# Six opening transfers on another queue, two norm sums two chunks later, and the mixers' last three units two steps later

## The reference

```python
for l in range(2):                                   # first block
    hn = rms_norm(h, norm_mix_g[l])
    q, k, v, xr, gate = split(hn @ w_in[l])
    o_attn = diff_attention(rope(norm(q)), rope(norm(k)), v, lam)
    o_rec = rg_lru_branch(xr, gate, ...)
    h = h + concat(o_attn, o_rec) @ w_out[l]
    hn = rms_norm(h, norm_ffn_g[l]);  h = h + (silu(g) * u) @ w_down[l]
for l in range(2):                                   # second block
    # mixer: short convolution, top-k attention ("d"), chunk-band attention ("c")
    mix = hybrid_mixer(x, positions, w_in[l], conv_w[l], rel_bias[l], w_mix_out[l])
    x = layer_norm(ALPHA * x + mix)
    cross = memory_cross_attention(x, mem, w_mq[l], w_mkv[l], w_mo[l])
    x = layer_norm(ALPHA * x + cross)                # the second norm
    x = layer_norm(ALPHA * x + squared_relu_mlp(x, w_ff1[l], w_ff2[l]))
```

## Time and profile before

| | before |
|---|---|
| time, three runs | 2864.87, 2864.66 and 2860.75 us (median 2864.66) |
| profiled execution | 2860.26 us, span 2858.5 us |
| TensorE busy | 2768.6 us, 97% of the span |
| VectorE, ScalarE, GpSimd busy | 1651.1, 1268.0 and 370.8 us |
| DMA | 85 GB/s on average |

### The profile page before, as it was taken

How to read it: one execution, slowest core, us unless ns; L and a number is a source line. 1 busy time by engine, 2 the same in 40 slices (tenths; PEclk the granted TensorE clock), 3 DMA queues, 4 the chain that set the end, 5 groups by cost and what they waited for, 6 DMA issues and landing times.

```text
span 2858.5 us, 39044 instructions
## 1 busy us (share of the span) xinstructions
PE 2768.6 (97%) x15748; PEld 2346.3 (82%) x15752; DVE 1651.1 (58%) x2479; ACT 1268.0 (44%) x2133; POOL 370.8 (13%) x291
## 2 busy tenths in 40 slices
PE   8999999999989999999999999999999999999997
PEld 7878999999877788887668888888776688888886
DVE  6786545454777745454876466333658764653335
ACT  5574322224674422233564545333445644443333
POOL 2222000001222000000223120000312231200003
PEclk9999999999999999999999999999999999999999
DMA  4112232232112233332123223323221232233332
GB/s 145 52 45 67 89 91 90 94 90 83 51 45 74 93 96 97 102 94 88 56 75 126 89 67 96 98 94 97 84 81 61 77 126 82 67 104 96 95 97 67
DMA packets 71923, 244.36 MB, mean 85 GB/s; under 512 B 9152, under 2 KB 10816, under 8 KB 71744
## 3 DMA queue, kind: packets, MB, share of 16 engines
q1 hardware_dynamic: 66528, 235.50, 25.7%
q10 hardware_dynamic: 5216, 6.36, 0.7%
HBM read 239.73 MB, written 2.10 MB: 85 GB/s over the span
## 4 chain that ended last, share of the span: by engine, by line
PE 83%; DVE 11%; ACT 3%; issue 2%; POOL 0%; DMA 0%; SPq 0%; ACTq 0%; DVEq 0%
PE psum L578 23%; PE psum L584 23%; PE psum L581 23%; PE psum L650 2%; DVE temp L2194 1%; DVE weights_hi_lo L1757 1%; PE psum L1080 1%; PE psum L673 1%; PE psum L675 1%; PE psum L1092 1%; PE psum L677 1%; DVE small L2192 1%; PE psum L907 1%; PE psum L935 1%; PE psum L960 1%
## 5 line engine op out<-in xcount | busy, mean ns | idle before, releaser
L578 PE MATMUL psum<-act_hi_lo,weights_hi_lo 128*128 128x264 f32 (+2 forms) x2544 | 776.3, 344 | 3.7 <-ACT temp L1290 2.8
L581 PE MATMUL psum<-act_hi_lo,weights_hi_lo 128*128 128x264 f32 (+2 forms) x2544 | 750.9, 334 | 1.9 <-DVE weights_hi_lo L1757 1.9
L584 PE MATMUL psum<-act_hi_lo,weights_hi_lo 128*128 128x264 f32 (+2 forms) x2544 | 752.1, 335 | 0.0
L1181 ACT ACTIVATE weights_hi_lo<-weights_float 128x1024 fp32r<-128x1024 f32 (+2 forms) x446 | 463.7, 1042 | 499.1 <-PE psum L584 430.7
L1757 DVE TENSOR_TENSOR weights_hi_lo<-weights_float,weights_hi_lo 128x1024 fp32r<-128x1024 f32 (+2 forms) x446 | 557.5, 1251 | 219.4 <-ACT weights_hi_lo L1181 218.1
L578 PE MATMUL psum<-hidden_hi_lo,weights_hi_lo 128*128 128x512 f32 (+2 forms) x1584 | 519.6, 358 | 3.7 <-DVE x_residual L2010 1.4
L584 PE MATMUL psum<-hidden_hi_lo,weights_hi_lo 128*128 128x512 f32 (+2 forms) x1584 | 511.6, 353 | 1.4 <-DVE hidden_hi_lo L2020 1.4
L581 PE MATMUL psum<-hidden_hi_lo,weights_hi_lo 128*128 128x512 f32 (+2 forms) x1584 | 511.2, 352 | 1.3 <-DVE weights_hi_lo L1757 1.3
L578 PEld LDWEIGHTS psum<-act_hi_lo,weights_hi_lo 128*128 128x128 f32 x2544 | 439.7, 189 | 68.3 <-issue 17.7
L584 PEld LDWEIGHTS psum<-act_hi_lo,weights_hi_lo 128*128 128x128 f32 x2544 | 438.4, 188 | 48.1
L581 PEld LDWEIGHTS psum<-act_hi_lo,weights_hi_lo 128*128 128x128 f32 x2544 | 438.0, 188 | 47.9 <-issue 2.6
(11 more groups left out here) (290 smaller groups left out, 3297.5 us busy)
## 6 DMA issues: line engine op xcount, KB each, us to landing
weights_float<-in_w_ff SPq DMA_DIRECT2D x128, 512.0 KB, 3.6
weights_float<-in_w_gu SPq DMA_DIRECT2D x88, 512.0 KB, 3.6
weights_float<-in_w_in SPq DMA_DIRECT2D x70, 512.0 KB, 3.6
weights_float<-in_w_down SPq DMA_DIRECT2D x32, 448.0 KB, 3.3
weights_float<-in_w_out SPq DMA_DIRECT2D x16, 512.0 KB, 3.6
weights_float<-in_w_down SPq DMA_DIRECT2D x16, 512.0 KB, 3.5
weights_float<-in_w_mv SPq DMA_DIRECT2D x16, 512.0 KB, 3.2
weights_float<-in_w_mix SPq DMA_DIRECT2D x16, 512.0 KB, 3.3
```

The costliest lines, as they stand in the source:

```text
L578: e.matmul(slot[:, place:place + c1 - c0], w_hi[:, col], x_hi[:, c0:c1], start=first, stop=False)
L581: e.matmul(slot[:, place:place + c1 - c0], w_lo[:, col], x_hi[:, c0:c1], start=False, stop=False)
L584: mm = e.matmul(slot[:, place:place + c1 - c0], w_hi[:, col], x_lo[:, c0:c1], start=False, stop=final)
L1181: e.activation(K.parts(n)[0][:, 0:cols], K.staged(n)[:, 0:cols], ACT.Copy).then_inc(*K.did("hi", n))
```

## The change

Three things. First, the six transfers (rotary tables, constants, the causal mask, lambda's vectors, the recurrent gates, the second block's parameters) go from ScalarE's queue to SP's, behind x and the first three w_v pieces and ahead of the fourth; GpSimd makes its masks behind the sums of squares; `small_before` stands behind all low parts of x, `scalar_small` at step 1 and `small_after` at step 2 of the first attention. Second, in `tiles_high_first` five chunks instead of three stand ahead of `between()`. Third, the "d" units with i = 3 stand two steps later, at 91, 94 and 96.

```diff
-          + [("d", p, i, 67 + (5 * n) // 2) for n, (i, p) in enumerate((i, p) for i in range(4) for p in range(3))])
+          + [("d", p, i, 67 + (5 * n) // 2 + (2 if i == 3 else 0)) for n, (i, p) in enumerate((i, p) for i in range(4) for p in range(3))])
...
-    high(group[:-1], order[:3])
+    high(group[:-1], order[:5])
     between()
     B.clear(2 * group[-1][1], 2 * group[-1][1] + 1)
-    high(group[-1:], order[:3])
-    high(group, order[3:])
+    high(group[-1:], order[:5])
+    high(group, order[5:])
...
     e.dma_start(m["x"][:, :, 0:META], t["meta_t"]).then_inc(*did("landed_meta", by=16))
     e.dma_start(m["par1"][:, :, :], t["params1"]).then_inc(*did("landed_params", by=16))
-    e.dma_start(m["rope"][:, 0:2, :], t["consts"][:, C_COS1:C_COLS].rearrange("p (a n) -> p a n", a=2)).then_inc(
-        *did("landed_rope", by=16))
-    e.dma_start(m["consts"][:, :], t["consts"][:, 0:C_CAUSAL]).then_inc(*did("landed_consts", by=16))
-    e.dma_start(K.once[:, 0:2 * P], t["consts"][:, C_CAUSAL:C_COS1]).then_inc(*did("landed_once", by=16))
-    e.dma_start(K.lams[:, 0:DEPTH * 4 * HEAD_DIM], t["lambdas"]).then_inc(*did("landed_lams", by=16))
-    e.dma_start(K.gates, t["w_gates"][0]).then_inc(*did("landed_gates", 0, by=16))
-    e.dma_start(m["par2"][:, :, :], t["params2"]).then_inc(*did("landed_params2", by=16))
...
     for s in range(STEPS1):
+        if l == 0 and s == 1:
+            scalar_small(e, w, K, 0)
         if s == 2:
...
     split_lo(e, w, K, 1)
     next_lo(e, w, K, "a", 0, 2)
-    small_before(e, w, K, 0)
     next_lo(e, w, K, "a", 0, 3)
     split_lo(e, w, K, 2)
     for k in range(4, DC):
         next_lo(e, w, K, "a", 0, k)
-    small_after(e, w, K, 0)
+    small_before(e, w, K, 0)
...
+        if l == 0 and s == 2:
+            small_after(e, w, K, 0)
         if s - 2 in UNIT_AT1[l]:
...
     square_sums(e, w, K, "a", 0, T1)
+    pool_masks(e, w, K)
     for l in range(DEPTH):
```

More of the change, by code:

```diff
@@ L1743, in scalar_program @@
     scalar_start(e, w, K)
-    scalar_small(e, w, K, 0)
     for l in range(DEPTH):
@@ L2491, in pool_start, with pool_masks @@
     e.memset(K.v[:, 4, :], 0.0).then_inc(*did("meta_zero"))
+def pool_masks(e, w, K):
+    m, did, done = K.m, K.did, K.done
     w.wait_ge(*done("landed_consts"))
@@ L2642, in sync_program @@
             load(c // 2)
+    e.dma_start(K.lams[:, 0:DEPTH * 4 * HEAD_DIM], t["lambdas"]).then_inc(*did("landed_lams", by=16))
+    e.dma_start(m["consts"][:, :], t["consts"][:, 0:C_CAUSAL]).then_inc(*did("landed_consts", by=16))
+    e.dma_start(K.gates, t["w_gates"][0]).then_inc(*did("landed_gates", 0, by=16))
+    e.dma_start(m["rope"][:, 0:2, :], t["consts"][:, C_COS1:C_COLS].rearrange("p (a n) -> p a n", a=2)).then_inc(
+        *did("landed_rope", by=16))
+    e.dma_start(K.once[:, 0:2 * P], t["consts"][:, C_CAUSAL:C_COS1]).then_inc(*did("landed_once", by=16))
+    e.dma_start(m["par2"][:, :, :], t["params2"]).then_inc(*did("landed_params2", by=16))
     for n in range(STAGING, len(PIECES)):
```

## The result

The changed kernel takes 2871.15 us in the median of 7 runs (2867.16 to 2872.71), the kernel before in the same comparison 2861.30 us (7 runs, 2859.14 to 2864.87). The ratio is 1.0027, with a 95% interval of 1.0017 to 1.0037: slower by 0.27%, some 8 us, or 9.9 us from median to median. The prediction was 2863.2 us, in 2856 to 2869; the time lies outside, on the slow side.

A forecast was written before the change was run, and what follows sets the result against it. TensorE, busy for 97% of the span, was taken as the bound, so time could come only from its idle stretches and clock. Start −2.2, norm −3.4, mixers +3.2, clock +3.0 gave +0.6 on 2862.6: 2863.2 us, range 2856 to 2869.

The forecast's parts named there:

- part 2: Second norm: eight more rows ahead of the sums remove TensorE's wait in both layers, −3.4 us (−2.5 to −3.5).
- The forecast of the sums: Second norm: 1.92 us of rows cover the 1.74 us idle, so the wait goes and the sums come 0.18 later.
- The correction: Behind w_ff1's first group: reads the squared mean and root many rows later, so the 0.18 us delay was given no cost.
- Part 3: Mixers: old waits go, −2.8 us a layer; a new 4.4 us wait for bank 0's emptying comes; both layers +3.2.
- Part 4: TensorE's clock: falls to half behind each new mixer wait, 1.5 us a layer, +3.0 us (0 to 5.5).
- Part 1: Start and first attention: earlier first matmul −1.2, fourth w_v piece's wait −1.1, later small operations +0.1, sum −2.2 us.
- The first matmul: Start: comes at 7.5 us instead of 8.70, a gain of 1.2 us (0.8 to 1.5).
- The tiny operations in the attention: First attention, step 2: `small_after`, 4.9 us on VectorE against 4.51 idle, costs TensorE +0.1 us, +0.4 without cover.
- The wait of L675: Fourth w_v piece: TensorE's 1.07 us wait for the low part behind `small_after` goes, −1.1 us.
- Rival 3: Mixers: half clock lasts 5.5 us instead of 3.4 at each of two places, +3.1, 2865.7 us; chance 0.2.
- the second low stretch of the earlier trace: At 2065.40 to 2070.90 us: half clock under full work for 5.50 us, taken as support for the longer half clock.
- all cases: The forecast (0.38) and four rivals: clock stays up 0.2, no new wait 0.12, longer half clock 0.2, start gains nothing 0.1.

The follow-up runs named there:

- the run of the norm alone: Only five chunks instead of three ahead of the second norm's sums, against the kernel before: 2865.79 us beside 2864.51, ratio 1.0007.
- the run with the weights early: Five chunks ahead of the sums plus w_ff1's fourth and fifth pieces made earlier, against the kernel before: 2860.01 us beside 2863.77, ratio 0.9987.
- the units' run: Only the three "d" units two steps later, against the kernel before: 2871.84 us beside 2864.51, ratio 1.0025.
- the run with the copies early: Units two steps later, with ScalarE's memory copies and bank 0's emptying moved earlier, against the kernel before: 2864.54 us beside 2863.77, ratio 1.0001.

## Why the prediction was wrong

**The step that failed is in part 2.** "What is later by that, the squared mean and the root on ScalarE and VectorE, is read by the correction behind w_ff1's first group, many rows later." The forecast of the sums was right: the wait of L1030 went, the sums came 0.2 later, and the ledger stands at −1.8 behind them. The correction was not late either (VectorE begins it at 1724.74 us, and at 1720.15 before, which is the ledger's 4.6 us at that place). But it was not the reader to look for. Behind the group stand the next tile's weights, piece 3 of w_ff1: ScalarE makes their high part behind five normed chunks, VectorE their low part behind that, and this chain begins with the sums. Before, TensorE came to the high part's row 0.27 us behind the end of L1181, and a row that waits comes 0.15 behind it, so 0.1 us was to spare there; and then it already waited 0.64 us for the low part: the chain had no slack at all. With the change it ends no earlier, since the sums begin it and VectorE's totals set the sums. TensorE only does 1.92 us of its work ahead of the sums instead of behind, and stands still for 1.55 us and 0.69 us later on. Both the run of the norm alone (wait and ledger) and the run with the weights early (wait gone, −1.3 instead of +1.5) show this. Instead of −1.7 a layer it is 0.0 for the waits and +1.5 for the clock behind the new one: +3.0 for −3.4.

**Part 3 was right to the tenth**: 4.36 + 0.05 expected, 4.40 measured, by the chain named. **Part 4** had the lower clock right at the mixers: 1.5 us a place expected, and the ledger's 3.1 and 3.4 less the waits' 1.6 leave 1.5 and 1.8. It was not asked for the norm, since there no wait was seen. Part 3 and 4 together: +6.2 expected; in the units' run +6.6 by the ledger, +7.3 by the medians.

**Part 1**: −2.2 expected; −1.6 by the traces' averages, −2.5 (±2.5) by the medians. The first matmul came 0.8 earlier on average and not 1.2. The tiny operations in the attention cost TensorE 0.3 us, at 51 us in all five traces with the changed start, and not 0.1. The wait of L675 is gone, but the 1.07 us of the earlier trace rows are not what every execution had: of the nine traces with the old start five have 1.0 to 1.1, two 0.4 and 0.8, and two none.

So with part 2 put right the sum should have read −2.2 + 3.0 + 3.2 + 3.0 = +7.0, and with the measured parts −1.6 + 3.0 + 6.6 = +8.0; the measured +8 to +10 differs from that by no more than what one program's medians differ between comparisons (2861.30, 2863.77 and 2864.51 for the kernel before). Rival 3 had the right side and the wrong reason: low stretches of 3.4 us, not 5.5, but at four places instead of two. Its model, the second low stretch of the earlier trace rows, came behind a wait of 6.1 us, which the prediction didn't look at. The range was too narrow since all cases shared the gain of part 2.

What stays open: why a moderate wait lowers the clock in one execution and not in another was not tried, and the medians can't settle the start's gain more closely than 0 to −5 us; the −1.6 rests on fourteen traces.

## What to carry to other kernels

Work pulled into a wait shortens nothing if the operation waited for also begins the chain to the next wait. Follow that chain to the engine's next rows that have a wait, weights included, and compare its slack with the work moved ahead (here 1.9 us). A wait that stands at the chain's end before the change (here 0.64 us) says that there is none. And on an engine with two clocks, price a new wait of 3 us or more as the wait plus half of the low stretch behind it (here 1.5 to 1.8 us for 3.4); a wait of 1.55 us among shorter ones cost the same here.

## What the runs showed of the hardware

The lower clock came behind every wait of 4.4 us (six in three traces) and of 3.1 us (two in one), and behind the norm's place each time (six in three traces), where a wait of 1.55 and further short ones left TensorE busy for 1.22 of 3.41 us in the row shown; not behind the 1.0 and 0.9 us of the run with the copies early. Each of these stretches lasted 3.4 us. Behind the wait of 6.1 us at 2059 to 2065 us, which all the kernels have, it was 6.8 us in thirteen traces and 10.2 in one. One program's traces had three and six places with a low stretch, with nearly the same waits in them, and that alone moved a trace by 5.4 us. At the start the higher clock began between 12.0 and 15.2 us of the span, with the first matmul between 7.5 and 9.0.
